# A one-core hybrid decoder trunk: router lots of one, two, four and one heads, a wider stretch from mixing to the query products, and output and query products in halves

## The reference

```
for l in range(2):
    sh1, sc1, g1, sh2, sc2, g2 = split(silu(c) @ w_ada[l] + b_ada[l], 6)
    y = token_mixer(rms_norm(x) * (1 + sc1) + sh1)     # ends: concat(three normed parts) @ w_out
    x = x + g1 * y
    h = rms_norm(x) * (1 + sc2) + sh2                  # 128 tokens x 1024 a tile
    q = h @ wq                                         # 8 heads x 2 sides x 128
    scores = q . subkeys                               # 8 heads x 2 x 128 keys
    top 16 of each side -> 256 sums -> top 16 -> expert index, softmax gate
    # per token: 8 heads x 16 experts, each expert a row u (1024) and a row v (1024)
    x = x + g2 * sum_k gate_k * gelu(h . u[e_k]) * v[e_k]
```

## Time and profile before

| | us |
|---|---|
| median of 3 runs | 3211.58 |
| lowest and highest run | 3205.68 and 3225.38 |
| profiled execution, its own time | 3208.42 |
| its span in the trace | 3206.6 |
| PE, VectorE, ScalarE, GpSimd busy | 2326.6, 2330.6, 1512.7, 1151.8 |
| bytes moved by DMA | 1303.66 MB |

### The profile page before, as it was taken

The page is one execution under the profiler, slowest core; times in us unless marked ns, Lnnn a source line. Parts: engine busy times, 40 slices in busy tenths (PEclk is TensorE's granted clock), DMA queues, the critical chain, the costliest instruction groups (busy, mean ns, idle before and its releaser), DMA issues.

```text
span 3206.6 us, 45259 instructions
## 1 busy us (share of the span) xinstructions
PE 2326.6 (73%) x15268; PEld 1177.7 (37%) x15268; DVE 2330.6 (73%) x6338; ACT 1512.7 (47%) x4895; POOL 1151.8 (36%) x1029
## 2 busy tenths in 40 slices
PE   7777778676875778757786677868687677875555
PEld 5463335242451434413243333524245143441111
DVE  6688766878668777777658776687867877688554
ACT  2325453445535455544544545444554545544443
POOL 0013333344433333333433433334443334334442
PEclk9888889888997988879798888978889899888777
DMA  9889999999999999999999999999999999999997
GB/s 363 360 316 415 412 419 390 421 419 413 418 412 417 417 414 388 418 420 419 409 402 419 418 419 403 408 421 420 415 411 411 420 418 413 401 416 417 421 421 328
DMA packets 204318, 1303.66 MB, mean 407 GB/s; under 512 B 26541, under 2 KB 42125, under 8 KB 52534
## 3 DMA queue, kind: packets, MB, share of 16 engines
q0 software_dynamic: 147456, 1073.81, 81.3%
q1 hardware_dynamic: 55910, 226.31, 17.7%
q10 hardware_dynamic: 720, 0.66, 0.1%
HBM read 1295.81 MB, written 7.16 MB: 406 GB/s over the span
## 4 chain that ended last, share of the span: by engine, by line
DMA 38%; PE 29%; DVE 17%; ACT 8%; issue 5%; POOL 3%; SPq 0%; ACTq 0%; DVEq 0%; POOLq 0%
DMA ringbuf<-in_p_uv,IDX 34%; PE PS L1084 14%; DVE ringbuf L1988 8%; PE PS L1000 3%; PE PS L835 3%; POOL ringbuf L685 3%; PE PS L1041 3%; ACT v_th L1447 2%; ACT v_w L1456 2%; DMA WB<-in_p_wi 2%; ACT DIAG L1463 2%; PE PS L765 1%; PE PS L912 1%; DMA WB<-in_p_ada 1%; DMA WB<-in_p_wq 1%
## 5 line engine op out<-in xcount | busy, mean ns | idle before, releaser
L685 POOL DMA_INDIRECT ringbuf<-in_p_uv,IDX x1024 | 1151.5, 1124 | 2027.3 <-PE PS L1084 1661.9
L1084 PE MATMUL PS<-ringbuf,DIAG 64*64 64x512 f32 x8192 | 1257.9, 741 | 740.5 <-ACT DIAG L1463 721.4
L1988 DVE SCALAR_TENSOR_TENSOR ringbuf<-ringbuf,H 128x1024 f32<-128x1024 f32 x1024 | 1236.8, 1222 | 572.8 <-DMA ringbuf<-in_p_uv,IDX 569.1
L1084 PEld LDWEIGHTS PS<-ringbuf,DIAG 64*64 64x64 f32 x8192 | 307.6, 155 | 1407.9 <-ACT DIAG L1463 960.8
L1444 ACT ACTIVATE v_sq<-v_y 128x2 f32<-128x2 f32 x512 | 104.2, 203 | 1305.3 <-DVE ringbuf L1988 1305.1
L1447 ACT ACTIVATE v_th<-v_sq,v_y 128x1 f32<-128x1 f32 x1024 | 340.5, 380 | 17.1
L1456 ACT ACTIVATE v_w<-v_th,v_g 128x1 f32<-128x1 f32 x800 | 265.9, 379 | 38.2 <-ACT v_th L1447 1.1
L1041 PEld LDWEIGHTS PS<-HT,WB 128*128 128x128 f32 x1920 | 233.1, 202 | 78.9 <-issue 44.4
L1041 PE MATMUL PS<-HT,WB 128*128 128x128 f32 x1920 | 244.3, 288 | 17.8 <-DMA WB<-in_p_wq 16.9
L1463 ACT ACTIVATE DIAG<-fold,v_w 128x64 f32<-128x64 f32 x800 | 234.6, 340 | 13.0
L835 PE MATMUL PS<-WB,HT 128*128 128x256 f32 (+2 forms) x816 | 175.8, 370 | 36.8 <-DMA WB<-in_p_wi 36.8
(11 more groups left out here) (325 smaller groups left out, 2429.2 us busy)
## 6 DMA issues: line engine op xcount, KB each, us to landing
WB<-in_p_wq SPq DMA_DIRECT2D x60, 1024.0 KB, 12.3
WB<-in_p_wi SPq DMA_DIRECT2D x37, 1024.0 KB, 9.6
ringbuf<-in_p_ahead SPq DMA_DIRECT2D x20, 1024.0 KB, 12.2
WB<-in_p_ada SPq DMA_DIRECT2D x16, 1024.0 KB, 15.3
ringbuf<-in_p_uv,IDX POOLq DMA_INDIRECT x1024, 12.3
WF<-in_p_ada SPq DMA_DIRECT2D x12, 1024.0 KB, 14.3
WB<-in_p_wi SPq DMA_DIRECT2D x14, 768.0 KB, 9.1
KEEP<-in_p_wo SPq DMA_DIRECT2D x8, 1024.0 KB, 19.7
```

Of the source, the lines that this page charges most:

```text
L685: pool.indirect_dma_start(out=ring[n % RING], out_offset=None, in_=table, in_offset=bass.IndirectOffsetOnAxis(ap=IDX[:, k % 2, s:s + 1], a ...
L1084: mm = pe.matmul(PS[half:half + HALF, 2 * c + r, :], DIAG[r * HALF:(r + 1) * HALF, (n + q) % DIAGS, :], row[r * HALF:(r + 1) * HALF, D + c ...
L1988: dve.scalar_tensor_tensor(row, row, GELU_T, H2[:, k % 2, :], ALU.mult, ALU.mult, accum_out=Y[:, b, q:q + 1]).then_inc(dotted, 1)
```

## The change

- The lots of tiles 1 to 7 become (1, 2, 4, 1). `LARGEST` is 4, the index buffers grow to 64 entries, and the placing costs of a lot (`LOT_COSTS`) now depend on its size; in a lot of four the index block is cut at one more place.
- `at` adds up to 3 pairs to every step from 34 to 42 in proportion, and 3 to every later one, except in tiles 0 and 3.
- The transposes of the mixed rows go to banks 6 and 7. The first spread row is made at step 33, ahead of them, and the second right after output chunk 2.
- Each output chunk and each query chunk is placed as two halves (`yield` in the middle), half a step and 0.75 step apart.
- In tiles 1 to 7 the scores of head i - 1 go ahead of the query products of head i, not behind them; ACT's query steps are half a step later, with the scores' copy first.
- `fold_sides` moves from before pair 1 to before pair 4 of a phase, and `finish` from after pair 2 to after pair 4.
- ACT places the gates of the tile before between later pieces, by their step.

```diff
-LARGEST = 3
-GROUPS_OF = [(1, 1, 2, 3, 1)] + [(2, 2, 3, 1)] * (TILES - 1)
+LARGEST = 4
+GROUPS_OF = [(1, 1, 2, 3, 1)] + [(1, 2, 4, 1)] * (TILES - 1)
...
-HEAD_COSTS, LOT_COSTS = (1.7, 1.7, 3.3), (1.0, 2.2, 3.4)
+HEAD_COSTS = (1.7, 1.7, 3.3)
+LOT_COSTS = {1: (1.0, 2.2, 3.4), 2: (1.0, 2.2, 3.4), 3: (1.0, 2.2, 3.4), 4: (1.2, 2.2, 1.0, 2.2, 1.8)}
...
+WIDER = 3
+FOLD_AT = 3
...
 def at(j, step):
-    return START[j] + step + (2 if step >= 4 else 0)
+    wider = 0 if j in (0, T - 1) else WIDER * min(1.0, max(0.0, (step - 34) / 8))
+    return START[j] + step + (2 if step >= 4 else 0) + wider
...
-                yield at(j, 34)
+                yield at(j, 33)
                 for c in more[-2:]:
                     ada_kept(pe, ada_number[c])
                 if j == 0:
...
+                else:
+                    pe.wait_ge(lmax, 12 * (j + 1))
+                    if l:
+                        pe.wait_ge(mod_in, 48)
+                    spread_row(0, 4).then_inc(rows_mm, 1)
+                yield at(j, 34)
+                pe.wait_ge(at_fin, 2 * (j + 1))
                 pe.wait_ge(mx_n, 3 * (j + 1))
                 for k in range(KD):
-                    last = pe.transpose(PS[:, 4 + k // 4, k % 4 * P:(k % 4 + 1) * P],
+                    last = pe.transpose(PS[:, 6 + k // 4, k % 4 * P:(k % 4 + 1) * P],
...
                     for k in range(KD):
+                        if k == KD // 2:
+                            yield at(j, 35.5 + i)
                         last = pe.matmul(PS[:, 6 + i % 2, 0:WIDE], HT[:, k, :], wt[:, k * WIDE:(k + 1) * WIDE],
...
+                    if j and i == 2:
+                        pe.wait_ge(g1_ev, j + 1)
+                        spread_row(1, 4)
...
                     yield at(j, 42 + 1.5 * i)
+                    if j and i >= 1:
+                        score(i - 1)
...
                     for h in range(2):
+                        if h == 1:
+                            yield at(j, 42.75 + 1.5 * i)
...
-                    if k > 0 and i == 0:
+                    if k > 0 and i == FOLD_AT:
                         fold_sides(k - 1)
...
-                    step = at(j, min(42.5 + 1.5 * i, 42 + 1.5 * PH))
+                    step = at(j, min(43 + 1.5 * i, 42 + 1.5 * PH))
...
+                    if nh == 4:
+                        yield
...
-                    if k > 0 and i == 2:
+                    if k > 0 and i == FOLD_AT + 1:
                         finish(k - 1)
```

More of the change, by code:

```diff
@@ L207, in route_clock @@
         clock.append([])
-        for cost in HEAD_COSTS * (h1 - h0) + LOT_COSTS:
+        for cost in HEAD_COSTS * (h1 - h0) + LOT_COSTS[h1 - h0]:
             step = ROUTE_AT + now / ROUTE_RATES[0] if now <= dense else ROUTE_TURN + (now - dense) / ROUTE_RATES[1]
@@ L215, in gate_clock @@
 def gate_clock(j):
-    return [lot[-len(LOT_COSTS)] for lot in route_clock(j)]
+    return [lot[-len(LOT_COSTS[h1 - h0])] for lot, (h0, h1) in zip(route_clock(j), early_lots(j))]
 def ada_rows(j):
@@ L992, in tile @@
                         pe.wait_ge(at_fin, 2 * (j + 1))
-                        if l:
-                            pe.wait_ge(mod_in, 48)
-                        if j:
-                            spread_row(0, 4).then_inc(rows_mm, 1)
                     if i >= 2:
@@ L1009, in tile @@
                 if j:
-                    spread_row(1, 4)
                     spread_row(2, 6).then_inc(rows_mm, 1)
@@ L1044, in tile @@
                     last.then_inc(w_done, 1)
-                    if i >= 1 and (j > 0 or i > 1):
+                    if j == 0 and i > 1:
                         score(i - 1)
@@ L1232, in tile @@
                     head(j, step)
-                if owed:
-                    yield last
-                    gates(j - 1, len(early_lots(j - 1)) - 1)
                 if j == 0:
@@ L1239, in tile @@
                 for i in range(1, 8):
+                    if owed and last <= at(j, 5 + i):
+                        owed = False
+                        yield last
+                        gates(j - 1, len(early_lots(j - 1)) - 1)
                     yield at(j, 5 + i)
@@ L1357, in tile @@
                         act.wait_ge(mx_tp, 2 * j + k // 4 + 1)
-                    act.activation(HT[:, k, :], PS[:, 4 + k // 4, k % 4 * P:(k % 4 + 1) * P], ACT.Copy,
+                    act.activation(HT[:, k, :], PS[:, 6 + k // 4, k % 4 * P:(k % 4 + 1) * P], ACT.Copy,
                                    scale=LP[:, LP_MIX + k:LP_MIX + k + 1]).then_inc(mx_ev, 1)
@@ L1387, in tile @@
                     yield step
+                    if j and i >= 1:
+                        score_ev(i - 1)
                     if i < PH:
```

## The result

The changed kernel takes 3240.49 us in the median of 4 runs (3239.18 to 3243.35), the kernel before 3213.65 in 4 runs on the same chip: a ratio of **1.0076, with a 95% interval of 1.0054 to 1.0097**. I had forecast 3202, 7 us of gain; it lost 24 us by the ratio and 27 by the medians.

A forecast was written before the change was run, and what follows sets the result against it. DMA at 421 GB/s was taken as the bound, with 49 us at most to win. Terms -12 - 1 + 0 + 5 + 1 = -7 us on the profiled 3208.4 gave 3201.4, forecast 3202 us; range 3184 to 3224.

The forecast's parts named there:

- What bounds the kernel: Whole kernel: DMA queues with a ceiling of 421 GB/s; 49 us in the steady part are all the change can win.
- Point 1: Wider steps and halves at the output projection, pairs 40 to 52: 12 us gained in six tiles, 1 in tile 3.
- the loop takes such a single bump: Output projection, place 41: PE's 7.5 us load, 2.5 over one pair, is made good within the next two.
- Points 2 and 3: Spread rows and banks: nothing beyond the projection's gain; query halves with scores first: 0, bounds 0 and 3 us.
- Point 4: New lots at phase starts: about 4 us left before first indices are needed; 0 lost, bound 3 us a tile.
- Point 5: Lot of four's end against the next tile's rotation and scans: 9.4 us DVE block, 5 us lost in five tiles.
- should mostly fit in the loop: At the lot of four's end, the ring absorbs 2 to 5 us of lateness; 1 us a tile lost, bounds 0 and 4.
- My sign for being wrong: Wrong if POOL waits for indices at phase starts, windows behind place 70 fall below 410, or output-projection windows don't rise.
- Point 6: Later fold_sides and finish: ACT waits 1 to 2 us at head for x's store; 1 us lost in all.
- That the loss only moves: Single bumps and a denser router at phase starts take back the 13 us: 3208, between 3203 and 3215; chance 0.28.
- The clock rival: Thinner PE work at the output projection leaves PE at its lower clock: 79 us lost, 3287; chance 0.03.
- The late-lot rival: POOL waits for first-lot indices at every phase start: 36 us lost, less the 13 won, 3231; chance 0.11.

The follow-up runs named there:

- experiment 4: Changed kernel with the last spread row due at step 39.5 instead of 40 in tiles 1 to 7: 1.0059 of the kernel before.
- experiments 9 and 13: Kernel before with output and query chunks in halves, nothing else: 1.0010; kernel before with output chunks alone in halves: 1.0011.
- experiment 15: Whole output chunks in tile 3, on the changed kernel with early fold, router rate 3.2, earlier last spread row and store: 0.9986 of the kernel before.
- experiment 16: No halves at all, wider steps kept, on the changed kernel with early fold, router rate 3.2, earlier last spread row and store: 0.9995.
- experiment 14: Kernel before with the query chunks alone in halves: 1.0019.
- experiments 3 and 10: Changed kernel with scores behind the query products again: 1.0096; kernel before with scores first and ACT's query steps half a step later: 1.0002.
- experiments 7 and 11: Changed kernel without extra pairs: 1.0065; kernel before with sums folded after pair 3 and x finished after pair 4: 1.0026.
- experiment 1: Changed kernel with sums folded after pair 1 and x finished after pair 2, not after 3 and 4: 1.0035 of the kernel before.
- experiment 6: Store of x ahead of tile 4's output-weight loads, on the changed kernel with early fold, router rate 3.2 and earlier last spread row: 0.9998.

## Why the prediction was wrong

- **What bounds the kernel: right.** Every loss is one of DMA rate, at places that the windows show; the sum by bytes meets the span to 2 us.
- **Point 1 (forecast -13): the place right, the balance wrong.** The six wider windows went from 20.1 us of loss to under 1, more than my 12. But 17.0 came back at pairs 52 to 56 and 4 in tile 3. The failed step is "the loop takes such a single bump": single bumps were to stay and to cost nothing. The one behind the projection costs 17.0 us. There the wider steps put the last spread row behind the pair that VectorE's add of chunk 3 delays, where it had stood ahead of it; moving it ahead again took back 11 of the 17 us (experiment 4). I had listed the places of the pieces on TensorE and not those of their partners on VectorE. The row and the norm that reads it fall due together (place 44.25), but so they did before (42); what changed is which pair stands between them and the add. The halves are shown to cost only where steps are not wide (experiments 9 and 13): of the 4 us in tile 3, whole chunks took back about half (experiment 15). In the wide tiles with the early row they cost nothing (experiment 16).
- **A slip in the same point.** By `at` the halves fall due at 37.4, 38.1, 38.8, 39.4, 40.1, 40.8, 41.5 and 42.2. So one half falls before the pair of place 38 and two before 39, not the other way round, and the trace has it so in tile 2. The sum over the six pairs is the same.
- **Points 2 and 3: right in sum.** On the kernel before, the order is measured at 1.0002 and the query halves at 1.0019. The halves alone do make TensorE wait more for query chunks, as I had said (77.9 us, experiment 14), but in the changed kernel it waits less (5.8 us): a wait that I had not seen, for ScalarE's query copy, 70.7 us, comes first, and costs nothing that can be told (experiments 3 and 10). The other banks, the first spread row's new place and the new order of the gates were never run alone.
- **Point 4: right.** POOL waits once; the lots alone are 1.0009.
- **Point 5 (forecast 5): mechanism right, mis-sized.** The block is 9.7 us against 9.4, in five tiles. It costs 2.6 to 3.3 us a tile and not 1, 14.4 in sum: "should mostly fit in the loop" was the wrong term. My sign for being wrong, windows behind place 70 under 410 GB/s, came true here, with 365 and 355 at pairs 20 to 24.
- **Point 6 (forecast 1): mis-sized, 12.5.** I had costed tile 2's path, with 8.8 us in hand, and carried it to all tiles. In tile 4 the store stands behind 4 MB and nothing was in hand: ScalarE waits 20.8 us, and pairs 4 to 12 of phase 3 lose 7.3 us more than before. The rest, some 5 us in the other phases, comes only with the wider steps (experiments 7 and 11); its way is open. The gap between fold and finish also shrank from two pairs to one, and VectorE waits for the fold in seven phases, but it shrank in experiment 1 too, where nothing is lost at pairs 4 to 8.
- **The rivals.** That the loss only moves, at 0.28, was the nearest, and half of it came: the bumps cost. The denser router at the start of the phase shows at most in the 5 us left open under point 6 (-0.1 us at pairs 0 to 4, -0.3 at 12 to 20). Its range ended at 3215. The clock rival is not seen as a whole (PE's mean is 0.866, before 0.862). The late-lot rival is out by POOL's row.

In sum: -15.5 + 17.0 + 14.4 + 12.5 + 1.2 for the rest is 29.6 us.

## What to carry to other kernels

When steps in a hand-written order are spread out, list for each moved piece the place of its partners on the other engines as well, and count the pairs between; here a row changed sides with a delayed pair, and a block that had stood two pairs ahead of another came to stand right before it. A path that hands over through a DMA queue must be costed in the tile where that queue is fullest. And before a stretch is relieved, ask what the next late thing is: of 19 us won in six tiles at one place, 17 were lost again in the four pairs behind it.

## What the runs showed of the hardware

- A block of 9.7 us on VectorE costs 2.6 to 3.3 us of DMA time in this ring of eight 1 MB buffers, so the ring took up 6 to 7 us of it; a wait of 20.8 us on ScalarE costs 5.6 in the four pairs where it falls.
- In tile 2 of the changed kernel, behind a gap of 3.70 us on TensorE, a pair takes 3.69 us in place of 1.95 and the spread row behind it 3.16 in place of 1.89: the granted clock is 0.50 in the windows from 892 to 898 us, the level of 1.2 GHz, and 1.00 from 901. Behind the gaps of 1.54 and 2.59 us at the same place in experiment 4 a pair took 1.95.
- The store of 512 KB behind 4 MB of loads landed 29.0 us after its issue, in the kernel before and in the changed one; put ahead of them (experiment 6) it took 11.4.
